# A decoder-block kernel: the weights of the start loaded in f32 on another queue, constants in regions of their own, and the late modulation units moved into the first stage

## The reference, cut to what matters

```python
c_act = jax.nn.silu(c)
mod = c_act @ w_ada[l] + b_ada[l]                      # (B, 6*D): shift1, scale1, gate1, shift2, scale2, gate2
h = modulate(rmsnorm(x, norm1_gain[l]), shift1, scale1)
proj = h @ w_in[l]                                     # q | k | v | u | vg | gate logits, 5632 columns
y_attn = sliding_window_attention(q, k, v, ...)        # window 128, 16 heads, 4 kv heads, ALiBi, sinks
u = gelu(u); vg = gelu(vg)
y_gmlp = chunked_spatial_gating(u, vg, ...)            # u * (W_s layernorm(vg) + b), chunks of 128
merged = g_attn * (y_attn @ w_o_attn) + g_gmlp * (y_gmlp @ w_o_gmlp)
x = x + gate1 * (merged @ w_out)
h2 = modulate(rmsnorm(x, norm2_gain), shift2, scale2)
x = x + gate2 * hierarchical_moe(h2, ...)              # top-1 of 4 groups, top-2 of 4 experts
```

## Time and profile before

| | us |
|---|---|
| median of 3 timed runs | 2296.0 (2286.13 to 2322.69) |
| the profiled execution | 2303.6 |
| its span, slowest core | 2302.0 |
| span of the other cores | 2236.3 to 2291.7 |
| TensorE busy | 1823.6 (79%) |
| VectorE busy | 1045.1 (45%) |
| ScalarE busy | 874.7 (38%) |

### The profile page before, as it was taken

How to read it: one execution, slowest core, us unless ns; L and a number is a source line. 1 busy time by engine, 2 the same in 40 slices (tenths; PEclk the granted TensorE clock), 3 DMA queues, 4 the chain that set the end, 5 groups by cost and what they waited for, 6 DMA issues and landing times. The chain is left out here.

```text
span 2302.0 us, 36156 instructions; the slowest of 8 cores (2236.3 to 2302.0 us)
## 1 busy us (share of the span) xinstructions
PE 1823.6 (79%) x10828; PEld 942.8 (41%) x11023; DVE 1045.1 (45%) x2275; ACT 874.7 (38%) x1364; POOL 484.8 (21%) x484
## 2 busy tenths in 40 slices
PE   0377799578879987977997887899748978879987
PEld 0233354245334435533544543444434434435443
DVE  0426454245745436565444574543563323224333
ACT  0324652035356316347524535641313323223322
POOL 1102000023201004210012320100413434324432
PEclk9989999779989999899999998999758989989999
DMA  7577437883538555354566442855329989789786
GB/s 110 127 158 104 101 72 146 153 262 126 90 86 157 126 157 203 84 119 90 117 157 223 138 78 74 179 112 137 133 88 288 213 232 207 178 208 205 130 207 101
DMA packets 114626, 338.04 MB, mean 147 GB/s; under 512 B 26660, under 2 KB 56748, under 8 KB 104196
## 3 DMA queue, kind: packets, MB, share of 16 engines
q0 software_dynamic: 67888, 196.56, 44.9%
q1 hardware_dynamic: 46548, 139.15, 17.7%
HBM read 543.67 MB, written 170.67 MB: 310 GB/s over the span
## 5 line engine op out<-in xcount | busy, mean ns | idle before, releaser
L167 PE MATMUL PS<-hT,slot 128*128 128x512 bf16 x2247 | 564.7, 395 | 62.2 <-DVE B L167 22.3
L167 PEld LDWEIGHTS PS<-hT,slot 128*128 128x128 bf16 x2304 | 224.9, 101 | 347.1 <-issue 113.6
L167 PE MATMUL PS<-slot,B 128*128 128x512 bf16 x1285 | 321.6, 391 | 35.8 <-DMA slot<-w_bf 25.7
L167 ACT ACTIVATE bfh<-PS 128x512 bf16<-128x512 f32 (+2 forms) x431 | 235.9, 590 | 104.8 <-PE PS L167 102.2
L167 PE MATMUL PS<-BB,slot 128*128 128x512 bf16 x984 | 240.5, 385 | 5.7 <-issue 5.2
L167 ACT ACTIVATE FH<-PS,cst 128x512 f32<-128x512 f32 x128 | 88.0, 687 | 311.0 <-PE PS L167 310.9
L167 PEld LDWEIGHTS PS<-slot,B 128*128 128x128 bf16 x1360 | 131.2, 101 | 175.3 <-issue 54.8
L167 ACT ACTIVATE B<-PS 128x1024 bf16<-128x1024 bf16 x79 | 80.9, 1024 | 287.2 <-PE PS L167 275.7
L167 POOL TENSOR_TENSOR small<-small 128x1 f32<-128x1 f32 x96 | 78.8, 821 | 525.5 <-DVE small L167 524.7
L167 DVE SCALAR_TENSOR_TENSOR bfh<-PS,small,FH 128x512 bf16<-128x512 f32 x79 | 59.3, 751 | 284.3 <-PE PS L167 277.3
L167 PE MATMUL PS<-slot,hT 128*128 128x512 bf16 (+1 forms) x759 | 155.9, 356 | 29.4 <-DVE kT L167 14.9
(11 more groups left out here) (176 smaller groups left out, 2484.6 us busy)
## 6 DMA issues: line engine op xcount, KB each, us to landing
slot<-w_bf SPq DMA_DIRECT2D x265, 512.0 KB
w_bf<-w_ch POOLq DMA_DIRECT2D x96, 512.0 KB
B4h<-w_bf SPq DMA_DIRECT2D x53, 512.0 KB
etab<-w_bf SPq DMA_DIRECT2D x52, 512.0 KB
kT<-w_bf SPq DMA_DIRECT2D x52, 512.0 KB
FH<-x SPq DMA_DIRECT2D x32, 512.0 KB
BB<-x SPq DMA_DIRECT2D x32, 512.0 KB
out<-BB SPq DMA_DIRECT2D x32, 512.0 KB
```

The costliest lines, as they stand in the source:

```text
L167: ins = getattr(eng, name)(*a, **k)
```

## The change

- The four first units of w_ada are loaded in f32 by plain DMAs on SP's queue, in halves of 1 MB, into the space of BB, hT and B3 (four staging buffers `stg`), and cast into slots by VectorE. u0, g0, g1 of w_in follow in the same way through stagings 0, 1 and 3; u1 and q0 stay with POOL's casting DMAs.
- x of stage 0 is loaded on ScalarE's queue, seven blocks at once, in seven buffers. The norm runs up to its transposes while w_ada arrives; `hT` is evacuated by ScalarE and VectorE in turns, between the casts.
- `r_const` is split: -0.5, the identity, A1/S1, WmT, R2, etab, the modulation's inputs.
- The small constants and the inputs of the spatial tables are issued behind w_ada (`rest_load`), the tables made in steps 0 and 1 of the gating part (`rest_ops`), the fills of vaug and kT done by POOL.
- Units 4 to 9 go through staging 3 and B4h and are worked one per gating step (`ada_load`, `ada_late`). Units 10 and 11 are cast by POOL's DMAs into B4h and worked at query products 4 and 10 (`ada_pool`). Nothing of w_ada is left between attention and output part, nor in the last stage.
- A cache store is put off (`pst`): one per gating step, or all ahead of the next fetches in attention, or when its slot is taken again.
- o0, o1 and u0 are fetched in stage 0 too after the first half of the attention outputs.

The diff, cut to its core:

```diff
+    def take_slot():
         i = scur[0] % NSLOT
+        if i in pst:
+            pst.pop(i)()
...
+    def f32_load(src, i):
+        for h in range(2):
+            t, tr = stg[i][h]
+            K.dma("sp", lambda e: e.dma_start(out=t.rearrange("p (k f) -> p k f", k=4),
+                                              in_=src[512 * h:512 * (h + 1), :].rearrange("(kc p) f -> p kc f", p=128)), reads=[], writes=tr)
...
+            K.op("dve", lambda e: e.tensor_copy(out=dst[:, 2048 * h:2048 * (h + 1)], in_=t), reads=list(tr), writes=[dst_r])
...
+    def ada_load(u):
+        f32_load(w_ada[:, 512 * u:512 * (u + 1)], 3)
...
+    def ada_pool(u):
+        ld(B4h[:], wview(w_ada, 512 * u, 512), q="pool", regs=(r_B4,))
...
+    for u in range(4):
+        f32_load(w_ada[:, 512 * u:512 * (u + 1)], u)
...
+        def x_in(b_):
+            xin, xin_r = xt[b_ % 7]
+            K.dma("act", lambda e: e.dma_start(out=xin, in_=x[b_ * 128:(b_ + 1) * 128, :]), reads=[], writes=xin_r)
...
+        xi = {b_: x_in(b_) for b_ in range(7)}
...
+        rest_load()
+        for i, key in enumerate(("u0", "g0", "g1")):
+            f32_load(w_in[:, (1536, 2560, 3072)[i]:(1536, 2560, 3072)[i] + 512], (0, 1, 3)[i])
...
+        for key in ("u1", "q0"):
+            fetch(key)
...
         if st == 0:
-            stage_A(0)
-            for key in ("u0", "g0", "g1"):
-                fetch(key)
-        fetch("u1")
-        fetch("q0")
+            first_norm()
+            late = ada_load(4)
...
+            if st == 0:
+                if 0 < s < 7:
+                    ada_late(3 + s, *late_b)
+                if s < 2:
+                    rest_ops(s)
+                if s < 6:
+                    for h in range(2):
+                        cast_half("dve", h, B4f, r_B4, 3)
+                    late_b = late
+                if s < 5:
+                    late = ada_load(5 + s)
+                if 2 <= s:
+                    flush_one()
+                if s == 4:
+                    rest_fill()
+        if st == 0:
+            rest_zero()
+            late = ada_pool(10)
...
         for key in ("q1", "k", "v", "br00o"):
             fetch(key)
+        if st == 0:
+            rest_etab()
...
+            if st == 0 and i == 4:
+                ada_late(10, *late)
+                late = ada_pool(11)
+            if st == 0 and i == 10:
+                ada_late(11, *late)
...
-        if st == 0:
-            ada_late_1()
-            ada_late_2()
-            fetch("o0")
-            fetch("o1")
...
-            g2w = [load_unit(wview(w_ada, 512 * u, 512)) for u in (10, 11)]
...
-            if last and i in (4, 6):
-                n_ = (i - 4) // 2
-                ada_rows([10 + n_], g2b[:, 512 * n_:512 * (n_ + 1)], r_g2, g2w[n_:n_ + 1])
```

More of the change, by code:

```diff
@@ L497, in build_nc @@
-    ld(wsf[:], wsT[:, :], regs=(wsf_r,))
-    mkt, mkt_r = f32h.next()
-    ld(mkt[:, 0:128], k_maskT[:, :], regs=(mkt_r,))
-    ld(bones[:], k_bones[:, :], q="pool")
-    ld(ones_bf[:], k_ones[0:1, :].rearrange("o p -> p o"), q="pool")
-    ld(etab[:, 0:2048], k_etab[:, 0:2048], q="pool")
-    ld(etab[:, 2048:4096], k_etab[:, 2048:4096], q="pool")
-    ld(triu[:], k_tri[:, :], q="pool")
-    ld(col[:], k_col[:, :])
-    ld(row[:], k_row.partition_broadcast(128))
-    r_c = Region("c_act")
-    K.op("act", lambda e: e.activation(out=CA, in_=CF, func=AF.Silu), reads=[r_c0], writes=[r_c0])
@@ L546, in build_nc @@
-    r_g1 = Region("g1b"); r_a2 = Region("a2s2"); r_g2 = Region("g2b"); r_mod = Region("modfm")
-    def ada_fm(units, lo_, hi_, pre=None):
-        mb, mbr = nb(1)
-        for n_, u in enumerate(units):
-            slot, sr = pre[n_] if pre is not None else load_unit(wview(w_ada, 512 * u, 512))
-            w8 = s8(slot)
-            for fl in range(4):
-                j = 4 * u + fl - lo_
-                for kc in range(8):
-                    K.op("pe", lambda e, kc=kc: e.matmul(
-                        bank(mb, 1, j), w8[:, kc, fl * 128:(fl + 1) * 128], c_bf[:, kc:kc + 1],
-                        start=(kc == 0), stop=(kc == 7)),
-                         reads=[sr, r_c], writes=mbr, inc=(kc == 7 and fl == 3))
-        K.op("dve", lambda e: e.tensor_tensor(out=modfm[:, lo_:hi_], in0=bank(mb, hi_ - lo_), in1=bfm[:, lo_:hi_], op=ALU.add),
-             reads=mbr + [r_const], writes=[r_mod])
@@ L563, in ada_rows @@
-    def ada_rows(units, dst, dst_r, pre=None):
-        for n_, u in enumerate(units):
-            slot, sr = load_unit(wview(w_ada, 512 * u, 512)) if pre is None else pre[n_]
-            w8 = s8(slot)
-            gb, gbr = nb(1)
-            for kc in range(8):
-                K.op("pe", lambda e, kc=kc: e.matmul(bank(gb), c_rep[:, kc, :], w8[:, kc, :], start=(kc == 0), stop=(kc == 7)),
-                     reads=[sr, r_c], writes=gbr, inc=(kc == 7))
-            bt, bt_r = f32h.next()
-            ld(bt[:], b_ada_row[0:1, 512 * u:512 * (u + 1)].partition_broadcast(128), regs=(bt_r,))
-            K.op("dve", lambda e: e.tensor_tensor(out=dst[:, 512 * n_:512 * (n_ + 1)], in0=bank(gb), in1=bt[:], op=ALU.add),
-                 reads=gbr + [bt_r], writes=[dst_r])
@@ new lines, in fm_mm @@
+    def fm_mm(w8, sr, mb, mbr, j0):
+        for fl in range(4):
+            for kc in range(8):
+                K.op("pe", lambda e, kc=kc: e.matmul(
+                    bank(mb, 1, j0 + fl), w8[:, kc, fl * 128:(fl + 1) * 128], c_bf[:, kc:kc + 1],
+                    start=(kc == 0), stop=(kc == 7)),
+                     reads=[sr, r_c], writes=mbr, inc=(kc == 7 and fl == 3))
+    def ada_load(u):
+        f32_load(w_ada[:, 512 * u:512 * (u + 1)], 3)
+        bt, bt_r = f32h.next()
+        ld(bt[:], b_ada_row[0:1, 512 * u:512 * (u + 1)].partition_broadcast(128), regs=(bt_r,))
+        nt = None
+        if u in (8, 9):
+            nt = f32h.next()
+            ld(nt[0][:], n2_row[0:1, 512 * (u - 8):512 * (u - 7)].partition_broadcast(128), regs=(nt[1],))
+        return bt, bt_r, nt
@@ L669, in rstd_pool @@
         K.op("pool", lambda e: e.tensor_tensor(out=ss, in0=ss, in1=small[:, 120:121], op=ALU.pow),
-             reads=[rr, r_const], writes=[rr])
+             reads=[rr, r_m05], writes=[rr])
         return ss, rr
@@ L1024, in body @@
                         conv_step()
[L1025 removed]
+            if j == 0:
                 fetch("o0")
```

358 lines of the change are left out of this document (219 added, 139 removed).

## The result

The changed kernel takes 2270.1 us (median of 4 runs), the kernel before beside it 2307.4 us; the ratio is 0.988, with an interval of 0.985 to 0.992. So it is 1.2% faster, some 27 us, where 52 us were forecast, and stays within 2%.

What follows compares the result with a forecast made beforehand. Three holes in TensorE's work in about the first 487 us were taken as the bound; 54 - 29 - 27 + 44 + 10 = 52 us won, 2296 - 52 = 2244 us, range some 2208 to about 2280.

Steps and rivals of the forecast that it cites:

- A, the start: Start up to g1: g1 ready at 80 us instead of 134.7, with loads at 3.13 us per MB; 54 us won.
- I take 7: Start: six constants issued on SP ahead of w_in, possible 2 to 24 us, taken as 7 us.
- turns of software and hardware queues: Start: SDMA engines alternate between both queue kinds, so g1 waits for q0's turn; otherwise g1 is 7 to 9 us earlier.
- B, the gating part: Gating part of stage 0: grows from 56.6 to 86 us, paced by TensorE's 9.7 us step; 29 us lost.
- rival 2: Gating part: the ada load-cast-reload chain sets the pace, 13 us a step, 20 us more, 2264 us; chance 0.20.
- The router wait: Gating part: router bias counted as 3.6 us behind a VectorE wait of 3.81 us.
- C, the query part: Query part: TensorE waits for unit 11, attention 78 us after the first query matmul instead of 50.9; 27 us lost.
- rival 1: Query part: its loads are hidden, unit 11 in before the tenth product; 2220 us; chance 0.20.
- D, the late stretch: Last attention output to first router transpose: 64.3 us falls to the 18 of stage 1 plus 2; 44 us won.
- E, the last stage: Last stage: VectorE's waits for b_ada rows and 16 matmuls go; 10 us won of at most 12.3.
- The cache stores: Gating part: 3 us of engine time each, counted as nothing, covered by 0.7 us; without cover 3 x 3 us.
- (3): Loads before attention: plain f32 reads much dearer than 3.13 us per MB; no win at 4.8, 2334 us at 6; chance 0.07.

Runs made afterwards that it cites:

- e11: Changed kernel with the six f32 loads of w_in issued on SP ahead of the constants; 2279.6 and 2285.0 us, no ratio.
- e12: Changed kernel with kT not cleared and vaug's memset on VectorE while it waits for w_in; 2273.9 us, ratio to the kernel before 0.987.
- e4: Changed kernel with the router-bias matmuls put into the last gating step; 2266.2 us, ratio to the kernel before 0.988.
- e5: Changed kernel with the matmuls of ada unit 11 put into the attention part, its load unmoved; 2247.6 us, ratio to the kernel before 0.977.
- e14: Changed kernel with no cache stores in the gating steps; 2297.5 us, ratio to the kernel before 0.994.
- e2: Changed kernel with ada units 4 to 11 back in their old places, new start, regions, late tables and put-off stores kept; 2295.8 us, ratio to before 0.997.
- e3: Changed kernel with the memsets of vaug and kT on VectorE instead of POOL, same place; 2274.3 us, ratio to the kernel before 0.988.

## Why the prediction was right and wrong

**A, the start.** Right in mechanism, 9 us too large: on core 6 g1 comes at 87.2 and came at 132.1 before, 44.9 us instead of 54; 7.2 of the 9 are g1 later than 80, the rest is that core 2 had been later. Three terms were mis-sized. The price: w_ada's last half was in at 45.8 and not at 41, 3.5 us per MB for the 12.06 MB instead of 3.13. Constants: "I take 7" after 41; they held SP from 31.4 to 50.6, so w_in went out 4.8 us after w_ada was in, 2.6 us later than 48 in all. From w_in's issue to g1, counted as 2 + 19.7 + 9 + 1.4 = 32.1 us, it took 36.6. That sum has POOL's cast of q0 beside w_in and leaves out that of u1, issued at 42.2; between 45.8 and 85.8, when g1's last half was in, the two took 35.5% of the 16 engines' time, 14.2 us where 9 were counted. The terms were also added up as if each held the next. e11 speaks against that: w_in issued 15.6 us earlier brought g1 only 4.8 earlier. 22.5 MB (w_ada, x, w_in and both casting loads) were in at 85.8, 3.7 us per MB from 3.5 on, so it looks as if the engines and not SP set g1; no run here took a load away, which would show it.

On the turns of software and hardware queues: the trace has w_in's issue at 50.6 beside POOL's load of q0 at 48.8 with the engines full (DMA share 0.98 in 48:70), which does not speak against the rule; no run here took q0's load away, so whether g1 waited for its turn stays open.

**B, the gating part.** This step failed. It took TensorE's step of 9.7 us as the pace because the chain's is about 9, so that "VectorE stays below" and nothing beside the first unit is waited for. The groups of B4h come 10.7, 9.0, 9.9, 15.7 and 11.8 us apart. The first three steps are TensorE's, as forecast. The fourth is not: VectorE stood 5.7 us for POOL's memsets, which are in no term, unit 8 was cast at 145.0, and TensorE waited 5.18 us and worked the next groups at the lower clock. The chain had no slack for it: a unit's second half lands 11.4 to 13.0 us after the issue where 9.4 was counted, so that without the memsets (e12) the cast waits for the load instead, and the last two steps are still 12.2 and 13.5 us on the mean. So rival 2's mechanism is there in two steps of five, at the price of about its 13 us a step, and TensorE's pace in three; over the five it is 11.4 us a step, and e11 adds that unit 4's load, not TensorE, says when they begin. The router wait was the second miss, 8.51 us for 3.81, and the matmuls behind it ran at the lower clock; moving it (e4) won 11.4 us. The result is 94.5 us from g1 to the first query product against 86. Behind that product stands the wait of 5.33 us for ScalarE, which the sum doesn't have; as q1 is late in any case, it probably costs nothing here.

**C, the query part.** Right in its main claim: unit 11 is late and TensorE waits, 23 us and not hidden (rival 1 is out). Mis-sized: 91.3 us instead of 78 from the first query product to attention. Unit 11 is in 76 us after it, counted as 66 to 68: k came 38 us after it instead of 35, v 48 instead of 40 and br00o 60 instead of 48 (their stores are at 219.7, 229.7 and 241.9). Unit 11's load could not even be issued before 216.8, as it goes into B4h, which unit 10's matmuls read at 213.5, behind the wait for q1. Behind unit 11 stand 15.2 us, not 10: the first group takes 3.57 us where others take 1.89, and two v products wait 2.3 us each for VectorE. The sentence "nothing covers it" was true of the order as it stood, and that was the point to dwell on: nothing needs unit 11 before the experts, and e5 shows that its matmuls can stand where its load is long in.

**D, the late stretch.** Right: 20.6 us on the mean, 44.3 won of 44 forecast.

**E, the last stage.** Right: 11.6 won, 10 forecast.

**The cache stores.** Costed at nothing, with the reason that 0.7 us of slack a step covers them, which 3 us would not fit in. No run shows a cost in the gating part (e14), though there POOL's memsets may hide it; the value lies in where they are issued: taken out of the gating steps they cost 17 us in the query part (79.5 to 96.8), and put off in e2 they cost 17 in the late stretch.

**Sum.** Marks on core 6 were missed by 7.2 (A), 8.5 (B) and 13.3 us (C), together 29.0; on core 6 attention starts at 273.0 instead of 244. On the means attention is 33.2 us later than forecast, and 7.0 of it came back in stages 1 to 3; with the smaller differences that is the gap between 52 forecast and 26 on the marks. The time lies inside the stated range, near its upper end, but not for the reason given for that end, a price of 4.4 us per MB: the waits missed above put it there. (By its own terms the lower end is 2214, not 2208.) Of the rivals, (1) is out by unit 11's wait, (2) came in part, as told under B, and (3) is out: up to g1 the loads cost 3.5 to 3.7 us per MB, not 4.8, and the change is not slower; only in the gating part a unit's 2.36 MB took 11.4 to 13.0 us, 4.8 to 5.5 per MB.

## To carry to other kernels

Work that was moved to fill a hole must be put where its data are long in, not where its load was moved to: the load and the matmuls are two decisions. When two chains are within 10% of each other (9.0 and 9.7 us a step here), don't take the longer one as the pace: a hiccup in either is paid at once, and a start made earlier in one is lost if the other begins no earlier (e11). When undoing a part of a change, look for what the rest of the change does to the old order: the put-off stores made the old late stretch 17 us longer.

## What the runs showed of the hardware

A VectorE instruction stood still for POOL's memsets: TENSOR_SCALAR of 128x1024 from f32 took 6.52 us from 131.56 to 138.08, beside MEMSETs of 2.26 and 3.94 us on POOL that ended at 137.54; its neighbours take 0.81, and in e3, with the memsets on VectorE itself, so does this one. All eight cores show the 6.52 us. The Trainium skill (SBUF — State Buffer, SBUF: two separate sides) says that a VectorE instruction in a 2-port mode and a GpSimd instruction use one pair of ports under an exclusive lock, held for a whole instruction. The trace agrees, with 5.7 us lost; by its times VectorE did not get on between the two memsets, as it ended behind the second. On VectorE the same memsets take 2.22 and 3.90 us, so POOL's were no slower, and nothing was won by giving them to POOL.

Behind the waits of 5.18 and 8.51 us TensorE works at the lower of its two clocks (1.2 GHz) for a while: the granted clock is 0.66 in 140:150 and 0.70 in 170:182, and a group of eight matmuls of 512 columns takes 3.57 us instead of 1.89:

```profile
140.00:150.00 10.00, 4.61 (x41) 2.32 (x43) 8.57 (x13) 0.00 (x0) 0.55 (x1) 0.66 0.85 256
160.00:170.00 10.00, 1.83 (x9) 1.87 (x9) 7.11 (x11) 0.00 (x0) 0.00 (x0) 0.68 0.39 138
170.00:182.00 12.00, 11.78 (x50) 6.04 (x51) 1.54 (x3) 2.28 (x4) 0.00 (x0) 0.70 0.00 1
```

(the columns are the stretch, its length, busy time and count of TensorE, weight loads, VectorE, ScalarE and POOL, the granted clock, the DMA share and GB/s). Moving the router bias, with its wait of 8.5 us, so won 11.4 us.

SP's issue of a 1 MB f32 load took 3.4 us with others outstanding (13.54 us for four at 3.49) and 0.9 in the gating part (1.80 for two at 96.39), so a DMA that stands behind such loads in SP's queue is issued late: the 22 constants of the start held SP from 31.4 to 50.6.
